# The last add of ten norm sums folded to 512 columns on VectorE, with one fp32 product with ones instead of two

## The reference

```python
def rms_norm(x, w):
    xf = x.astype(jnp.float32)
    y = xf * lax.rsqrt(jnp.mean(xf * xf, axis=-1, keepdims=True) + EPS)
    return (y * w.astype(jnp.float32)).astype(x.dtype)
...
h = h + jnp.concatenate([ya, yb], axis=-1) @ w_out[l]
gate = jax.nn.sigmoid(rms_norm(h, ple_norm_w[l]) @ w_ple_gate[l] + b_ple_gate[l])
h = h + gate * (p[l] @ w_ple_proj[l])
return rms_norm(h, final_norm_w)
...
h = rms_norm_2(x, pre1_w[l]) * (1.0 + sc1) + sh1
...
x = x + (1.0 + gt1) * rms_norm_2(y, post1_w[l])
h = rms_norm_2(x, pre2_w[l]) * (1.0 + sc2) + sh2
y = swiglu_ffn(h, ffn_w_in[l], ffn_w_out[l])
```

## Time and profile before

| | |
|---|---|
| runs | 2177.2, 2178.34 and 2384.88 us, median 2178.34 us |
| profiled execution, span from first to last instruction | 2176.7 us |
| around the span, to the median of the runs | 1.6 us |
| TensorE busy | 98% of the span |
| VectorE, GpSimd, ScalarE busy | 53%, 54%, 33% |
| granted TensorE clock | 0.998 of full speed |

### The profile page before, as it was taken

The page is one execution under the profiler, slowest core; times in us unless marked ns, Lnnn a source line. Parts: engine busy times, 40 slices in busy tenths (PEclk is TensorE's granted clock), DMA queues, the critical chain, the costliest instruction groups (busy, mean ns, idle before and its releaser), DMA issues.

```text
span 2176.7 us, 29202 instructions
## 1 busy us (share of the span) xinstructions
PE 2141.6 (98%) x11096; PEld 1742.3 (80%) x11096; DVE 1149.8 (53%) x1413; ACT 710.6 (33%) x878; POOL 1179.3 (54%) x1096
## 2 busy tenths in 40 slices
PE   7999999999999999999999999999999999999997
PEld 5788887887777878777888888887888888888886
DVE  7988874367553261271389145735673344444207
ACT  6663333335533142121123241234442222212112
POOL 3342223566652232232486244466678888867776
PEclk9999999999999999999999999999999999999999
DMA  5324414232331111111223244443754455445343
GB/s 215 106 97 171 170 65 147 76 107 79 129 122 39 59 50 58 68 39 68 96 99 125 92 140 145 142 148 126 260 213 154 154 202 174 154 164 187 132 155 126
DMA packets 93601, 275.16 MB, mean 126 GB/s; under 512 B 8512, under 2 KB 19008, under 8 KB 93504
## 3 DMA queue, kind: packets, MB, share of 16 engines
q1 hardware_dynamic: 81152, 254.97, 33.6%
q10 hardware_dynamic: 12352, 18.88, 2.3%
HBM read 221.38 MB, written 52.43 MB: 126 GB/s over the span
## 4 chain that ended last, share of the span: by engine, by line
PE 88%; DVE 5%; ACT 2%; DMA 1%; SPq 1%; POOLq 1%; DVEq 1%; POOL 1%; issue 1%; ACTq 0%
PE PG L825 38%; PE PG L831 19%; PE PG L1412 14%; PE PG L1326 6%; PE PX L825 2%; PE PX L831 1%; PE PX L1055 1%; PE PX L1050 1%; DVE PX L2223 1%; PE PG L926 1%; DVE WK L2217 1%; PE PX L1033 1%; PE PX L1070 1%; PE PX L1003 0%; SPq L577 0%
## 5 line engine op out<-in xcount | busy, mean ns | idle before, releaser
L825 PE MATMUL PG<-UL,WH 128*128 128x512 f32 x1696 | 661.2, 390 | 0.0
L825 PE MATMUL PG<-UH,WH 128*128 128x512 f32 x1568 | 625.3, 399 | 4.5 <-ACT WK L2031 1.3
L706 POOL TENSOR_TENSOR TOUCH<-TOUCH 128x2 f32<-128x2 f32 x184 | 55.6, 302 | 829.8 <-PE PG L831 690.9
L709 POOL TENSOR_TENSOR WL<-WRAW,WH 128x1024 fp32r<-128x1024 f32 (+1 forms) x184 | 436.0, 2369 | 30.2 <-issue 30.2
L831 PE MATMUL PG<-UH,WL 128*128 128x512 f32 x1568 | 400.5, 389 | 0.0
L825 PEld LDWEIGHTS PG<-UL,WH 128*128 128x128 f32 x1696 | 318.6, 188 | 67.7 <-issue 3.8
L825 PEld LDWEIGHTS PG<-UH,WH 128*128 128x128 f32 x1568 | 294.3, 188 | 81.4 <-issue 11.2
L831 PEld LDWEIGHTS PG<-UH,WL 128*128 128x128 f32 x1568 | 294.4, 188 | 61.6
L707 POOL TENSOR_SCALAR WH<-WRAW 128x1024 fp32r<-128x1024 f32 (+1 forms) x184 | 188.7, 1025 | 0.0
L1412 PE MATMUL PG<-TH,AH 128*128 128x512 f32 x352 | 137.0, 389 | 0.3 <-POOL AL L755 0.3
L1412 PE MATMUL PG<-TH,AL 128*128 128x512 f32 x352 | 136.9, 389 | 0.0
(11 more groups left out here) (584 smaller groups left out, 3858.6 us busy)
## 6 DMA issues: line engine op xcount, KB each, us to landing
ADA<-ada_w SPq DMA_DIRECT2D x24, 1024.0 KB, 5.2
W2RAW<-down_w SPq DMA_DIRECT2D x48, 512.0 KB, 3.3
RAW<-up_w SPq DMA_DIRECT2D x22, 1024.0 KB, 6.2
WRAW<-out_w SPq DMA_DIRECT2D x30, 512.0 KB, 3.2
WRAW<-zg_w SPq DMA_DIRECT2D x24, 512.0 KB, 3.3
gates<-STG ACTq DMA_DIRECT2D x24, 512.0 KB, 2.6
WK<-gates SPq DMA_DIRECT2D x24, 512.0 KB, 3.4
WRAW<-up_w SPq DMA_DIRECT2D x22, 512.0 KB, 3.3
```

Source lines behind the costliest of these rows:

```text
L706: pool.tensor_tensor(TOUCH[:, 0:2], TOUCH[:, 2:4], TOUCH[:, 4:6], ALU.add)
L709: pool.tensor_tensor(WL[:, r, 0:n], WRAW[:, r, 0:n], WH[:, r, 0:n].bitcast(F32), ALU.subtract).then_inc(w_split, 1)
L825: mm = pe.matmul(out, w[:, r, at + P * k:at + P * k + P], v, start=first and k == ks[0] and n == 0, stop=False)
```

## The change

The last of the three adds (`u` = 3) becomes three adds of 512 columns in a new function `folded_add`: the accumulated columns 512 to 1023 onto 0 to 511, then, after the wait, the left half of the last square, then its right half. All three call sites use it. `half_sum` has one product of 512 columns left. Nothing else is changed.

```diff
             def half_sum(acc, ready, count):
 
                 pe.wait_ge(ready, count)
-                pe.matmul(PX[:, SUM_BANK, :], ONES[:], WK[:, acc, 0:512], start=True, stop=False)
-                pe.matmul(PX[:, SUM_BANK, :], ONES[:], WK[:, acc, 512:1024], start=False, stop=True).then_inc(norm_ms, 1)
+                pe.matmul(PX[:, SUM_BANK, :], ONES[:], WK[:, acc, 0:512], start=True, stop=True).then_inc(norm_ms, 1)
...
+            def folded_add(acc, y, ready, count, made):
+                folded = WK[:, acc, 0:512]
+                dve.tensor_tensor(folded, folded, WK[:, acc, 512:1024], ALU.add)
+                dve.drain()
+                dve.wait_ge(ready, count)
+                dve.tensor_tensor(folded, folded, y[:, 0:512], ALU.add)
+                dve.drain()
+                dve.tensor_tensor(folded, folded, y[:, 512:1024], ALU.add).then_inc(made, 1)
+                dve.drain()
+
             def pair_add(h, u, ready, count, acc, made):
 
+                if u == 3:
+                    folded_add(acc, y2(h, u), ready, count + 4 * h + u + 1, made)
+                    return
                 dve.wait_ge(ready, count + 4 * h + u + 1)
...
             def out1_acc(h, u):
+                if u == 3:
+                    folded_add(OUT1_ACC, WK[:, u, :], post_sq, 4 * h + u + 1, post_acc)
+                    return
...
             def post_add(h, u):
+                if u == 3:
+                    folded_add(POST_ACC, WK[:, POST_SQ + u % 3, :], post_sq, 16 + 4 * h + u + 1, post_acc)
+                    return
```

## The result

| | before | changed |
|---|---|---|
| median of ten runs | 2177.4 us | 2182.5 us (2181.1 to 2183.6) |
| ratio to before | | 1.0024, interval 1.0016 to 1.0033 |
| span of the profiled execution | 2176.7 us | 2181.5 us |
| granted TensorE clock, mean | 0.998 | 0.996 |

The account below looks back on a forecast made before the run. TensorE, busy 98% of the span, was taken as the bound. Terms +1.5 (through the fourth sum), +2.1, 0.0, -0.7, -0.86, -0.86, -0.6 gave +0.6 on 2178.3: forecast 2178.9 us, range 2172.5 to 2182.5.

Parts of the forecast that it names:

- The turns with GpSimd: VectorE's adds and GpSimd's weight splits lock each other out; a waiting add ends about 0.55 us after GpSimd lets go.
- sum 2: Second of ten sums in program order: product starts 0.31 us late, net -0.55 us.
- sum 3: Third of ten sums in program order: product at 504.94 instead of 504.09, net 0.0 us.
- sum 4: Fourth of ten sums, no slack: third add 3.9 us later behind GpSimd's turns, net +2.95 us.
- sum 5: Fifth of ten sums, where TensorE already waited 1.56 us: VectorE +3.05 us, 0.96 back, net +2.1 us.
- sum 6: Sixth of ten sums in program order: product 0.9 us late, net 0.0 us.
- L707 ahead of the second add: At sum 4 GpSimd's L707 follows L706 directly, before VectorE's second add: 3.9 us later rather than 1.5.
- sums 9 and 10: Last two of ten sums: cover taken like the eighth's at the ninth, a little at the tenth; -0.86 and -0.6 us.
- The adds at their own length: Rival: no extra GpSimd turns, VectorE's extra 1.02 us counts at sums four and five alone; 2172.6 us, chance 0.15.
- the full gain: Rival: TensorE's whole 8.6 us come out, as if VectorE's chain had slack; 2169.7 us, chance 0.03.
- VectorE slipping in behind L706: Rival: at sum 4 VectorE's second add takes the gap after L706, +0.6 instead of +2.95; 2176.6 us, chance 0.25.
- The slower case: Rival: third adds at sums five and six also meet the next tile's L709, 2.4 us each; 2183.7 us, chance 0.22.

Follow-up runs that it names:

- the kernel with the product alone: Kernel before with one product at every sum and its old 1024-column adds: 2172.7 us, ratio 0.9982 to before.
- the fifth sum alone: Kernel before with the change (folded adds, one product) at the fifth sum only: 2181.1 us, ratio 1.0018 to before.
- the PSUM kernels: Sums 3 to 6 accumulate in PSUM; changed at eight sums 2172.3 us, at all ten 2172.5, with wide adds and two products at 3 to 6 2174.3.
- The filled waits: Changed kernel plus four unused products ahead of TensorE's wait at the fourth sum and five at the fifth: 2178.5 us, ratio 1.0009 to before.
- at sum 5 alone: Kernel with the change at the fifth sum only, plus five unused products ahead of TensorE's wait there: 2178.4 us, ratio 1.0006 to before.
- the kernel with the adds alone: Changed kernel's folded adds at all ten sums, but two products in every sum: 2188.8 us, ratio 1.0056 to before.
- the fourth sum alone: Kernel before with the change (folded adds, one product) at the fourth sum only: 2181.8 us, ratio 1.0022 to before.

## Why the prediction was right or wrong

**Right: what a product costs, and who is late.** The second product was 0.86 us wherever TensorE set the pace: in the kernel with the product alone the steps behind sums 1, 2, 7 and 8 are -0.86, -0.86, -0.86 and -0.87 us. The turns with GpSimd came as worked out, sum by sum. Predicted and seen wait of TensorE beyond its old arrival: sum 2 0.31 and 0.3, sum 3 0.85 and 0.9, sum 4 3.9 and 3.85. For sum 5, VectorE 3.05 later was forecast and 3.2 seen (3.0 with the fifth sum alone); for sum 6, 0.9 and 0.8. The waits at the sums came to 9.9 us where I had said about 11, and the thirty short adds to a mean of 1.45 us where I had said above 1.2. At sum 4 the choice I had to make, L707 ahead of the second add, was the right one, by 0.05 us. The Trainium skill's exclusive lock (SBUF — State Buffer, SBUF: two separate sides) holds in both directions, and the PSUM kernels show its other half: the same section names VectorE instructions with two SBUF inputs as those that take the lock, and with one SBUF input VectorE is not held here (0.69 us).

**Wrong: the size.** I forecast +0.6 us, as good as nothing, and it is +5.1, clear of zero. That the time lies just inside the upper edge of my range of 2172.5 to 2182.5 owes something to the base: I started from 2178.3, the median of three runs, and the ten runs give 2177.4, from where the same range would have ended at 2181.6. Two terms of the sum failed.

The first is the work behind the new waits: the terms of sum 4 (+2.95), sum 5 (+2.1) and sum 6 (0.0) counted the waits and priced all that follows at full clock, so the slower clock stood at nothing, without a reason. The granted clock was 0.50 behind both waits, and that costs 3.4 us by the rows: 1.0 on the chain that leads to sum 5, where the product lasts 2.08 us instead of 1.02, and 2.4 behind sum 5, half of the 4.7 us that TensorE works there at 0.50. The filled waits gave back 3.5 us, at sum 5 alone 2.7. I had 3.9 and 4.6 us of waiting in my own sum and never asked what a wait of that length does to the engine. Around the change the profile before has no wait longer than 1.56 us, but at the start of the program it has one, and TensorE's rows behind it were there to be read:

```profile
9.42 0.77 PE L960 MATMUL PG<-UH,WH 128*128 128x512 f32 x1 [9.42 <-DVE UL L2272]
9.98 0.63 PE L960 MATMUL PG<-UL,WH 128*128 128x512 f32 x1
10.41 0.63 PE L960 MATMUL PG<-UH,WL 128*128 128x512 f32 x1
...
19.14 0.40 PE L960 MATMUL PG<-UL,WH 128*128 128x512 f32 x1
```

Behind 9.42 us of standing still the starts are 0.43 us apart until 18.5 us, the pace of the rows at 0.50, and 0.23 us apart from then on. The clock column reads 1.00 there and does not give it away; the matmuls' own rows do. The Trainium skill says that an idle TensorE falls to its lower clock (TensorE: Matmul & The Clock Gate, Part 1: The HAM clock gate); the rows at 0.50 agree, and the sum was made without it.

The second is the gain at sums 9 and 10. I counted -0.86 and -0.6, both without a row: sum 9 I took to be like the eighth. Measured alone they give 0.1 us the other way. Slack of VectorE ahead of the product was all that I asked for, and not what waits behind it: at sum 9 the product had covered the wait for ScalarE, at sum 10 the folded adds met a turn of GpSimd, and the unit behind it waits in any case. 3.4 + 1.5 is 4.9 us, and the forecast missed by 4.5; the difference is small beside the intervals.

**The rivals.** The adds at their own length (2172.6) and the full gain (2169.7) fall by the first rows after. VectorE slipping in behind L706 (2176.6) did not happen. The slower case gave 2183.7, near the measured time, by a mechanism that did not occur: the third adds of sums 5 and 6 stood free at 0.69 us. It would be wrong to call that a hit.

## What to carry to other kernels

Ahead of a saving on the busiest engine, ask two things of each place: who is queued with a wait before it, and what the engine would wait for right behind it; a product that covers another wait is free already. Here a vector add with two SBUF inputs cost up to one turn of GpSimd per instruction, so that one add split into three met up to three turns, and the adds with one input in PSUM met none. And the new idle stretches of 3.6 to 4.8 us on TensorE had half-clock matmuls behind them here; such a stretch is to be priced with them too, not only with its own length.

## What the runs showed of the hardware

The clock did not fall behind every long wait. In the profile of the kernel with the adds alone TensorE waited 3.42 us at sum 4 and its two products and the matmuls behind them ran at the full clock, while behind 3.61 us (the changed kernel) and 3.66 us (the fourth sum alone) they ran at half. These are single executions, and the mean granted clock of that kernel's five runs goes from 0.994 to 0.997, so the same wait need not end the same way twice; where the line lies is not shown. TensorE's rows of the adds-alone kernel:

```profile
527.07 1.12 PE L823 MATMUL PX<-WK,ONES 128*128 128x512 f32 x2 [3.42 <-DVE WK L2226]
528.03 1.02 PE L824 MATMUL PX<-WK,ONES 128*128 128x512 f32 x2
...
529.12 0.40 PE L831 MATMUL PG<-UL,WH 128*128 128x512 f32 x1
```

And filling the two waits with work that nobody reads was worth 3.5 us by the ratios, with nothing else changed.
